# Expert rows picked from x1 on the chip by products, in place of stored rows gathered by DMA

## The reference

```python
x = x + gt1 * rmsnorm(y, norm_gains[l, 1])          # called x1 in the kernel
h = rmsnorm(x, norm_gains[l, 2]) * (1.0 + sc2) + sh2
...
for e in range(N_EXPERTS):
    hid = jax.nn.silu(t @ w_up1[e]) * (t @ w_up3[e])
    y = y + combine[:, e:e + 1] * (hid @ w_down[e])
```

## Time and profile before

| | |
|---|---|
| median of 3 runs | 1177.38 us (1177.34 to 1177.88) |
| profiled execution | 1177.78 us, its span 1175.6 us |
| PE busy | 1033.6 us, 88% of the span |
| DVE, ACT, POOL busy | 385.5, 260.0, 171.3 us |
| granted clock, mean | 0.975 of full |
| moved by DMA | 281.64 MB |

### The profile page before, as it was taken

One profiled execution on the slowest core, in us unless ns is written; L12 is line 12 of the kernel. 1 busy time (PEld: TensorE's weight loads), 2 busy tenths in 40 slices (PEclk: granted clock), 3 DMA queues, 4 the chain that ended last, 5 costly groups with the idle time before them and its releaser, 6 DMA issues.

```text
span 1175.6 us, 16600 instructions
## 1 busy us (share of the span) xinstructions
PE 1033.6 (88%) x6906; PEld 522.5 (44%) x6906; DVE 385.5 (33%) x810; ACT 260.0 (22%) x407; POOL 171.3 (15%) x222
## 2 busy tenths in 40 slices
PE   3899999999998999999999699997888877777886
PEld 1578644466555676544446433332333322223231
DVE  1322566455447442114215522121111111111114
ACT  2342350076552222233024000000000000000004
POOL 0345100013320100000100111211101111111002
PEclk9799999999999999999999799999989999999999
DMA  9443404443320002325434799999999999999995
GB/s 325 151 148 121 143 1 143 143 144 108 115 100 37 3 4 75 109 90 198 173 128 172 274 400 394 402 398 406 405 405 407 405 406 411 392 399 402 412 412 222
DMA packets 71184, 281.64 MB, mean 240 GB/s; under 512 B 9754, under 2 KB 19244, under 8 KB 46554
## 3 DMA queue, kind: packets, MB, share of 16 engines
q1 hardware_dynamic: 63408, 265.94, 58.3%
q0 software_dynamic: 5120, 8.40, 2.3%
q10 hardware_dynamic: 2602, 6.52, 1.5%
HBM read 276.62 MB, written 12.60 MB: 246 GB/s over the span
## 4 chain that ended last, share of the span: by engine, by line
PE 51%; SPq 29%; DMA 7%; DVE 5%; ACT 4%; issue 2%; POOL 1%; ACTq 0%; POOLq 0%; DVEq 0%
SPq L388 20%; PE ps L1589 7%; SPq L392 5%; PE ps L1470 5%; PE ps L1900 4%; SPq L396 3%; PE ps L1600 2%; PE ps L1483 2%; DMA ring<-in_w_up 2%; PE ps L1484 2%; PE ps L1485 2%; PE ps L1836 2%; PE ps L1846 2%; PE ps L1515 2%; PE ps L1808 2%
## 5 line engine op out<-in xcount | busy, mean ns | idle before, releaser
L1900 PE MATMUL ps<-arena 128*64 128x512 f32 x672 | 151.8, 596 | 34.8 <-DMA arena<-in_w_up 34.8
L1356 DVE TENSOR_TENSOR arena<-arena,ps 128x256 f32<-128x256 f32 x32 | 13.5, 422 | 371.0 <-ACT arena L903 371.0
L1589 PE MATMUL ps<-arena,ring 128*128 128x512 f32 x256 | 118.6, 604 | 0.1
L1900 PEld LDWEIGHTS ps<-arena 128*64 128x64 f32 x672 | 49.0, 137 | 136.3 <-issue 105.1
L1915 PE MATMUL ps<-arena 128*64 128x512 f32 x336 | 84.9, 651 | 19.7 <-DMA arena<-in_w_down 15.0
L1900 PE MATMUL ps<-ring,arena 128*64 128x512 f32 x352 | 80.8, 603 | 14.6 <-DMA ring<-in_w_up 14.6
L903 ACT ACTIVATE arena<-ps 128x256 f32<-128x256 f32 x32 | 12.3, 384 | 259.2 <-PE ps L1900 259.2
L1351 DVE TENSOR_SCALAR arena<-ps,par 128x64 f32<-128x64 f32 x256 | 67.2, 335 | 5.0 <-PE ps L1889 5.0
L1589 PEld LDWEIGHTS ps<-arena,ring 128*128 128x128 f32 x256 | 46.1, 190 | 49.0 <-issue 47.2
L910 ACT ACTIVATE arena<-ps 128x512 f32<-128x512 f32 x32 | 19.1, 597 | 187.7 <-PE ps L1915 187.7
L535 POOL TENSOR_SCALAR_AFFINE_SELECT arena<-arena 128x128 f32<-128x128 f32 x64 | 32.4, 539 | 186.3 <-DVE arena L1091 168.5
(11 more groups left out here) (354 smaller groups left out, 1463.6 us busy)
## 6 DMA issues: line engine op xcount, KB each, us to landing
arena<-in_w_up SPq DMA_DIRECT2D x84, 1024.0 KB, 29.9
ring<-in_w_up SPq DMA_DIRECT2D x44, 1024.0 KB, 28.4
ring<-in_w_down SPq DMA_DIRECT2D x11, 2048.0 KB, 34.7
arena<-in_w_down SPq DMA_DIRECT2D x11, 2048.0 KB, 32.1
ring<-in_w_mod SPq DMA_DIRECT2D x10, 2048.0 KB, 9.4
arena<-in_w_down SPq DMA_DIRECT2D x20, 1024.0 KB, 28.0
ring<-in_w_in SPq DMA_DIRECT2D x6, 2048.0 KB, 8.7
ring<-in_w_in SPq DMA_DIRECT2D x8, 1024.0 KB, 9.0
```

What stands on the lines that cost most here:

```text
L1589: last = mm(ps[:, bank, :], w[:, k, P * (n % 2):P * (n % 2) + P], hT[:, k, :], start=(k == 0), stop=(k == KD - 1))
L1900: last = mm(ps[64 * hf:64 * hf + 64, UP_BANK[u], :].rearrange("p (m n) -> p m n", m=2), hgT[:, k, :], up_pair(u, k)[:, :, 256 * hf:256 * h ...
```

## The change

No row of h is stored, no list of rows is made and nothing is gathered. x1 stays in SBUF, and the rows of a block are picked from it by a product. For each block DVE makes a matrix of tokens by slots, `pick_w` (128 tokens by 64 slots for each of 4 token tiles): it holds a token's inverse root mean square where that token sits in that slot of that block, and zero elsewhere. It comes from `slot_key`, which holds the block number plus one of the slot that a token's choice has (`pick_of_block`: one comparison with `block_no` and one sum over the two choices). PE multiplies it with x1 (`pick_rows`, 8 products of 512 moving columns, into the bank that the block's up will use), ACT copies the 128x512 result to `picked` (`picked_rows`), and PE turns it by 16 products of 64x64 with the identity (`turn_rows`). The hidden transposes become `turn_hidden`. The first block's `pick_w` is made ahead of the eight masks. The products with the last block's weights (`selw`) go from ahead of the loop to behind it, and the overflow list is made later, with a second step of `route_ready` for SyncE. GpSimd keeps only the scatters. Set 2's down matrix is loaded whole with the first halves of its up matrices.

```diff
-        hrow = [S(14, 1)[0:CAP, 0:D], S(14, 1)[0:CAP, D:2 * D], S(13, 1)[0:CAP, D:2 * D]]
+        slot_hot, slot_tmp, slot_key = (S(14, 1)[:, 512 * i:512 * i + 512].rearrange("p (n s) -> p n s", s=CAP) for i in range(3))
+        pick_w = S(14, 1)[:, 1536:1792].rearrange("p (t s) -> p t s", t=NT)
+        picked = S(13, 1)[:, 1024:1536]
...
-            sp.wait_ge(h2_stored, 16 * NT)
-            sp.dma_start(eset_down[2][1], first_down[:, 1, :]).then_inc(w_in_sem[2][2], 16)
...
-            for u in range(NSET):
-                gather_rows(u, idx_i[:, u:u + 1])
...
-                    pool.wait_ge(hg_done, NSET * it + (u + 1))
-                    nc.gpsimd.tensor_copy(idx_now[:, u:u + 1], idx_i[:, bass.ds(NSET * it + (NSET + u), 1)]).then_inc(idx_link, 1)
-                    pool.wait_ge(idx_link, NSET * it + (u + 1))
-                    pool.sem_inc(register_pass, 1)
-                    gather_rows(u, idx_now[:, u:u + 1])
...
-                link(A(h2tok[:, t % 2, :], x1[:, t, :], ACT.Copy, scale=V("rs", 8 + t)))
-                act.dma_start(h2_dram[P * t:P * t + P, :], h2tok[:, t % 2, :]).then_inc(h2_stored, 16)
...
+            def picked_rows(u, count):
+
+                act.wait_ge(pick_done, count)
+                A(picked, ps[:, UP_BANK[u], :], ACT.Copy).then_inc(picked_out, 1)
...
             for u in range(NSET):
                 silu_out(u, u + 1)
+                picked_rows((u + 1) % NSET, u + 2)
                 rows_out(u, u + 1, None)
...
+            picked_rows(1, NSET * again + (NSET + 2))
+            act.wait_ge(idx_done, 2)
+            A(selT, ps[:, 7, :], ACT.Copy).then_inc(selT_ready, 1)
...
-            TT(R(1168, 512, N2), io[:, :, 0:CAP].broadcast_to((P, N2, CAP)), o1(rr).broadcast_to((P, N2, CAP)), ALU.is_equal)
+            link(TT(slot_hot, io[:, :, 0:CAP].broadcast_to((P, N2, CAP)), o1(rr).broadcast_to((P, N2, CAP)), ALU.is_equal))
+            mine = rt[:, 264:264 + N2]
+            link(STT(mine, blk_, 0.0, rstd8, ALU.is_equal, ALU.mult))
+            link(TT(slot_tmp, slot_hot, o1(mine).broadcast_to((P, N2, CAP)), ALU.mult))
+            TT(pick_w, slot_tmp[:, 0:NT, :], slot_tmp[:, NT:N2, :], ALU.add).then_inc(sel_made, 1)
...
+            def pick_of_block(steps_before):
+
+                dve.wait_ge(sel_step, steps_before)
+                STT(slot_tmp, slot_key, block_no[:, 0:1], o1(rstd8).broadcast_to((P, N2, CAP)),
+                    ALU.is_equal, ALU.mult).then_inc(sel_step, 1)
+                dve.wait_ge(sel_step, steps_before + 1)
+                TT(pick_w, slot_tmp[:, 0:NT, :], slot_tmp[:, NT:N2, :], ALU.add).then_inc(sel_made, 1)
...
                     expert_dve(u, it)
                     rows_turned_in(NSET * it + (u + 2))
+                    TS(block_no[:, :], block_no[:, :], 1.0, None, ALU.add).then_inc(sel_step, 1)
+                    pick_of_block(2 * NSET * it + (2 * u + 3))
...
+            def pick_rows(u, count):
+
+                pe.wait_ge(sel_made, count)
+                for t in range(NT):
+                    for hf in range(2):
+                        last = mm(ps[64 * hf:64 * hf + 64, UP_BANK[u], :], pick_w[:, t, :], x1[:, t, 512 * hf:512 * hf + 512],
+                                  start=(t == 0), stop=(t == NT - 1))
+                last.then_inc(pick_done, 1)
+
+            def turn_rows(count):
+
+                pe.wait_ge(picked_out, count)
+                pe.sem_inc(register_pass, 1)
+                for k in range(KD):
+                    for a in (0, CAP):
+                        last = mm(ps[a:a + CAP, 0, CAP * k:CAP * k + CAP], picked[a:a + CAP, k::KD], ident[a:a + CAP, a:a + CAP],
+                                  start=True, stop=True, skip_group_check=True)
+                last.then_inc(hg_done, 1)
+
+            pick_rows(0, 1)
+            turn_rows(1)
...
-            def turn_rows(u, count):
-                pe.wait_ge(hrow_in[u], count * 16)
-                pe.sem_inc(register_pass, 1)
-                hv = hrow[u].rearrange("p (q k) -> p k q", k=KD)
-                for k in range(KD):
-                    last = tr(ps[:, 0, CAP * k:CAP * k + CAP], hv[:, k, :], ident[0:CAP, 0:CAP])
-                last.then_inc(hg_done, 1)
...
+            expert_up(0, 0)
             pe.wait_ge(route_ready, 1)
...
+            with pe.Fori(0, steps) as it:
+                for u in range(NSET):
+                    pick_rows((u + 1) % NSET, NSET * it + (u + 2))
+                    turn_hidden(u, it)
+                    turn_rows(NSET * it + (u + 2))
+                    expert_down(u, it)
+                    expert_up((u + 1) % NSET, it + (1 if u + 1 == NSET else 0))
+            pick_rows(1, NSET * steps + 2)
+            turn_hidden(0, steps)
+            turn_rows(NSET * steps + 2)
             pe.wait_ge(sel_ready, 2 * NT + 1)
...
-            with pe.Fori(0, steps) as it:
-                for u in range(NSET):
-                    expert_up(u, it)
-                    turn_rows((u + 1) % NSET, it + (1 if u + 1 < NSET else 2))
-                    expert_down(u, it)
```

More of the change, by code:

```diff
@@ L552, in _ @@
             pool.wait_ge(merged_ready, KD)
[L553 to L564, removed]
+            nc.gpsimd.memset(none, 0.0).then_inc(none_zero, 1)
             def scatter_rows(u, index):
@@ L1312, in _ @@
                 TS(ohb[:, i, :], K("iota64")[:, 0:MAXB], blk_[:, i:i + 1], K("dest")[:, i:i + 1], ALU.is_equal, ALU.mult).then_inc(sel_ready, 1)
+            lt6, over, moved, key8 = rt[:, 280:280 + MAXO // NSET], rt[:, 288:289], rt[:, 289:290], rt[:, 272:272 + N2]
+            link(TT(lt6, K("blk18")[:, 0:MAXO:NSET], ends[:, E - 1:E].broadcast_to((P, MAXO // NSET)), ALU.is_lt))
+            link(nc.vector.tensor_reduce(over, lt6, AX, ALU.add))
+            TS(nblk_i[0:1, 0:1], rt[0:1, 288:289], float(LOOPED // NSET), None, ALU.add)
@@ new lines, in _, with rows_turned_in @@
+            TS(nblk_i[0:1, 20:21], rt[0:1, 288:289], float(LOOPED // NSET - 1), None, ALU.add).then_inc(route_ready, 1)
+            link(TS(moved, over, float(NSET), -float(MAXO), ALU.mult, ALU.add))
+            link(TS(key8, blk_, float(LOOPED + MAXO), moved, ALU.is_ge, ALU.mult))
+            link(STT(key8, key8, 1.0, blk_, ALU.add, ALU.add))
+            def rows_turned_in(count):
+                dve.wait_ge(hg_done, count)
+                for k in range(KD):
+                    last = TS(hgT[:, k, :], ps[:, 0, CAP * k:CAP * k + CAP], V("A1", k), V("SH1", k), ALU.mult, ALU.add)
+                last.then_inc(hg_ready, 1)
@@ L1314, in _ @@
+            def pick_of_block(steps_before):
[4 more added lines that the diff above has]
+                TT(pick_w, slot_tmp[:, 0:NT, :], slot_tmp[:, NT:N2, :], ALU.add).then_inc(sel_made, 1)
+            rows_turned_in(1)
             dve.wait_ge(idx_done, 1)
-            second, where = rt[:, 300:300 + MAXB], rt[:, 360:360 + MAXB]
+            where = rt[:, 360:360 + MAXB]
@@ L1316, in _ @@
             link(TS(where, ps[:, 3, 0:MAXB], float(NOWHERE), None, ALU.add))
-            link(TS(second, where, float(T), -float(T), ALU.is_ge, ALU.mult))
-            TT(idx_i[:, :], where[0:CAP], second[0:CAP], ALU.add).then_inc(idx_ready, 1)
-            ov = ovb
+            TS(dst_i[:, :], where, 2.0, K("half"), ALU.mult, ALU.add).then_inc(dst_ready, 1)
+            link(TT(slot_key, slot_hot, o1(key8).broadcast_to((P, N2, CAP)), ALU.mult))
+            nc.vector.memset(block_no[:, :], 2.0).then_inc(sel_step, 1)
@@ L1324, in _ @@
+            over_e = rt[0:1, 300:300 + MAXO]
+            link(nc.vector.tensor_reduce(over_e.rearrange("p (m o) -> p m o", o=1), ovb[0:1], AX, ALU.add))
             link(TS(over_e, over_e, float(E - 1), None, ALU.min))
[L1325 to L1333, removed]
+            CP(nblk_i[0:1, 1:2], rt[0:1, 288:289])
+            CP(nblk_i[0:1, 2:2 + MAXO], over_e).then_inc(route_ready, 1)
             dve.wait_ge(gsum_ready, 1)
@@ L1878, in _ @@
                     for hf in range(2):
-                        last = mm(ps[64 * hf:64 * hf + 64, 3, 0:MAXB], ohr[:, t, :], selb[:, ch, t, :], start=(ch == 0 and t == 0),
-                                  stop=(ch == 1 and t == NT - 1))
+                        last = mm(ps[64 * hf:64 * hf + 64, 3, 0:MAXB], slot_hot[:, NT * ch + t, :], selb[:, ch, t, :],
+                                  start=(ch == 0 and t == 0), stop=(ch == 1 and t == NT - 1))
             last.then_inc(idx_done, 1)
-            idle_products(2)
-            def turn_rows(u, count):
-                pe.wait_ge(hrow_in[u], count * 16)
-                pe.sem_inc(register_pass, 1)
-                hv = hrow[u].rearrange("p (q k) -> p k q", k=KD)
-                for k in range(KD):
-                    last = tr(ps[:, 0, CAP * k:CAP * k + CAP], hv[:, k, :], ident[0:CAP, 0:CAP])
-                last.then_inc(hg_done, 1)
             def expert_up(u, it):
```

60 lines of the change are left out of this document (22 added, 38 removed).

## The result

The changed kernel takes 1222.98 us (median of four runs, 1220.74 to 1223.52), the kernel before 1177.63 in the same rounds: a ratio of 1.0381, with a 95% interval of 1.0363 to 1.0399. The profiled execution took 1223.02 us, with a span of 1221.2. The forecast was 1188.5, in a range of 1180 to 1206: slower was right, the size was not. The change costs 45 us where 11 were forecast.

The account below looks back on a forecast made before the run. Transfers bound the loop at 16.18 us a block; PE would take over at 15.69. 672.3 + 30 x 15.69 + 10.2 + 33.7 = 1186.9 us of span, +11.3, so 1188.5 us, range 1180 to 1206.

Parts of the forecast that it names:

- What bounds the kernel, and what comes in its place: Expert loop: transfers bound it at 16.18 us a block; after the change PE does, at 15.69, from its first block.
- Pick, down, up: PE's products in each block of the loop: pick 3.43 us, down 3.65, up 6.87.
- ahead of the loop: Stage before the expert loop: first up starts at 665.3 and ends at 672.3 us against 677.95, 5.7 earlier.
- the end: After up of block 30: 10.2 us instead of 5.7 through down, then 33.7 instead of 37.2 to the span's end.
- The gap: Between pick and turn in each block, PE waits for ACT's copy from PSUM: 0.71 us.
- The turn: PE's 16 products of 64x64 on the picked rows in each block: 1.03 us, 0.93 plus 0.10 for the stride.
- upper bound of 1.84: Highest price given for a block's turn, in us, if its 32 loads don't overlap at all.
- The sum: Whole kernel: 672.3 + 30 x 15.69 + 10.2 + 33.7 = 1186.9 us of span, 11.3 over the kernel before.
- The block at which it decides, 15.31: Loop block time in us at which the span equals the old 1175.6; below it the changed kernel is faster.
- The rival of the dearer turn: Loop: turn of 1.84 gives 16.5 us a block and 1213; a 0.3 wait gives 1197; chance of 1197 or more 0.20.
- The rivals' 1162: Loop stays transfer-bound: PE's work hides (chance 0.08) or the pick is cheaper (0.02, inside that); about 1162 us.
- The rate that the Trainium skill gives: Pick at 131 ns a product would take 2.1 us, loop some 40 us cheaper; not adopted, 0.215 a record kept.

Follow-up runs that it names:

- e6: Changed kernel with each block's pick moved one block ahead, so ACT's copy runs beside down and up; turn still strided by 8: 1211.76 us.
- e7: Changed kernel with the pick one block ahead and ACT's copy laying rows out so the turn reads neighbours: 1179.61 us, ratio 1.0013 to the kernel before.
- e1: Changed kernel with ACT's copy writing picked rows slot index innermost, so the turn reads without a stride: 1190.14 us, ratio 1.0104 to the kernel before.
- e11: Changed kernel with pick in rounded float32, halves in two PSUM banks, turn as eight transposes from neighbours: 1148.79 us, ratio 0.9748 to the kernel before.
- b1: Kernel before with only its first three gathers, so 30 blocks use wrong rows: 1150.96 us, ratio 0.9771 to the kernel before.

## Why the prediction was wrong

- **What bounds the kernel, and what comes in its place** (right). The bound was the transfers; PE took it over in the changed kernel from the first block on, with no wait for a weight in the loop and the clock at 1.00.
- **Pick, down, up, ahead of the loop, the end** (right). Pick 3.46 (forecast 3.43), down 3.58, up 6.87. From down of block 30 to the end of the span 32.8 (33.7). First up ends at 672.80 (672.3), which is partly luck: its first turn took 1.0 more than forecast, but the chain to it had begun 1.0 earlier, with the 0/1 matrix at 652.42 and not at 653.45. The terms there also add up to 664.9 for the start of up, and not to the 665.3 that stands. The scatter landed in 2.39 us, with the transfer engines 9% busy from 1188 to 1194 us:

```profile
1188.41 0.02 issue
...
1190.26 2.39 DMA choice_rows<-arena,dst_i
```

- **The gap** (nearly). 0.77 for 0.71.
- **The turn** (the step that failed). "I take 0.93 plus 0.10, since the columns are read with a stride of 8; a strided load of 128 columns takes 200 ns where an unstrided one takes 187." Measured 2.14 (2.07 in e6, where nothing is waited for ahead of it), above even the upper bound of 1.84. The base was 0.15 to 0.22 short: without the stride the turn is 1.08 in e7 and 1.15 in e1. The 0.10 was wrong by a factor of ten (2.14 - 1.15 = 0.99), and the flaw is in the pair of rows behind it: L1550 is not L1889 without a stride but another operation, a full float32 product with two records, where a transpose has one. e11 has the right partner, the same eight transposes from neighbours: loads of 138 ns in place of 200, and 0.68 us in place of 1.03. The stride's price was 62 ns a load and stood hidden in the old turn; in a load of 64 columns it is 78 (135 to 213). Both prices could have been read from the trace of the kernel before, in the view of the earlier trace rows:

```profile
L1818 PEld LDWEIGHTS ps<-cst,arena 128*128 128x128 f32 x32 | 3.7, 141 | 2.5 <-issue 2.3 <-DVE arena L1260 0.2
L1418 PEld LDWEIGHTS ps<-cst,arena 128*64 128x64 f32 x64 | 7.5, 216 | 2.6 <-issue 2.5
```

L1818 transposes x1 from neighbours, 141 ns a load beside the 200 of L1889. L1418 is a product whose stationary columns are read with a stride of 8, 216 ns beside the 137 of L1900, whose loads have the same form without one. Each pair differs in something else too (128 rows for 64; one moving column for 512), but both point to 59 to 79 ns where I had 13. And 1.84 was no upper bound: the 32 loads followed one another every 0.065 us (2.07 / 32), where it had 0.0575, half of the old 0.129 less a drain. Half of 0.129 as it stood gives 2.06, but that may be chance: from neighbours the same halving of 0.68 / 8 gives 1.36, and e7 measured 1.08.
- **The sum**: 30 x (16.81 - 15.69) = 33.6, all but 1 us of what the time was off. With the turn at its measured price the forecast's sum stands. (The upper end of 1196 for blocks of 15.4 to 15.9 comes to 1195; nothing hangs on it.) With a turn near the price that I had put on it, e1, the kernel takes 1190.14, 1.6 from the forecast.
- **The block at which it decides, 15.31** (borne out). e7 has 15.40, by that rule 2.7 us over the kernel before; measured +1.2 in the medians.
- **The rival of the dearer turn** (chance 0.20, 1197 and more) is the one that came. Its largest figure, 1213 with a turn of 1.84, was still 10 us short, and it named loads that don't overlap, not the stride.
- **The rivals' 1162** (wrong by 11 to 15). I had 0.42 us a block for a gather by the time of its packets and 0.32 by its bytes; both undercount what it takes from the others. Without it the stream runs at 421 GB/s in place of 404, and the block is 15.25 in place of the 15.76 to 15.86 I had written. Had PE been cheap enough, 1147 to 1151 was there to win, and the prediction undersold the idea of the change while it had the direction right for this form of it.
- **The rate that the Trainium skill gives** ("TensorE: Matmul & The Clock Gate", Back-to-back issue gap, about 131 ns a product with 512 columns). The trace does not agree: the pick ran at 0.216 us a record (3.46 / 16), as the rows said.

What stays open: why a gather takes 0.93 us from the stream when by the packets' busy share it is 0.42 and by its bytes 0.32; b1 takes away the gather's reads, its writes and its issue together. Open, too, is why a stride makes a load longer; the runs show the price and where it sets in, not the reason.

## What to carry to other kernels

Before pricing an operand that is read with a stride, find two rows of the same operation with and without it (here they stood in the view that was read), or treat the price as unknown; where a copy stands ahead of TensorE anyway, let it do the reordering, since it cost nothing on ACT. A wait of one engine is not free time: look at what already lies in it before you count it as a gain. Price an indirect transfer by taking it away and looking at the stream around it, not by the busy share of its own packets; and when work moves from the transfers to TensorE, what counts is whether the whole block fits under the transfers' pace, which here took a cheaper pick, of rounded float32, and not only a better turn.

## What the hardware showed that I had not expected

- For full float32, the stationary load of the turn's 64 columns takes 135 ns with elements 4 or 8 bytes apart and 213 ns at 16 or 32 bytes; a record with a moving operand of 512 columns takes 592 ns with neighbours and 1098 at 32 bytes.
- A load of 128 columns takes 138 ns from neighbours and 202 with a stride of 32 bytes in a transpose (e11 and the kernel before), and 187 to 190 from neighbours in a full float32 product (L1550, L1589), so loads are only compared within one kind of operation.
- ACT's copy of 128x512 from PSUM takes 0.61 us both with and without the stride of eight in its reading.
- Eight products of 128x64 by 512 in rounded float32 take 2.01 us in place of 3.46 for the same eight in full float32. The latter show two records a product, one every 0.216 us, the former one record, every 0.251; whether that comes of the half of the array's columns that each product writes (partitions 0 and 64 up, against 0 alone) wasn't tried.
- A gather of 0.13 MB (4.2 MB in 32 of them) slows a full weight stream by 0.93 us (16.18 a block with it, 15.25 without).
